# A new head for a two-layer transformer trunk: identity on chip, x and the first weights in quarters, fewer warm-up products

## The chip, the cores and the metric

The kernel runs on one core of one Trainium2 chip. A core has a matrix engine (TensorE, PE in the profile), a vector engine (VectorE, DVE), an activation engine (ScalarE, ACT), a general engine (GpSimd, POOL) and a sequencer that issues transfers (SyncE, SP); 16 DMA engines move data. The metric is the time of one launch on the device in microseconds (us), as the median of several runs. Lower is better.

## The reference

A trunk of two layers on 256 tokens of width 1024, all in float32. Each layer is a half SwiGLU sub-layer, a token-mixing sub-layer of two attentions, and another half SwiGLU. The change touches the first SwiGLU of the first layer alone:

```python
for l in range(DEPTH):                       # DEPTH = 2
    x = x + 0.5 * swiglu(rms_norm(x, ffn1_norm[l]), ffn1_w_gate[l], ffn1_w_up[l], ffn1_w_down[l])
    h = rms_norm(x, mix_norm[l])
    proj = h @ w_in[l]
    ...                                      # windowed attention A, latent attention B
    merged = sigmoid(g_a) * (o_a @ w_branch_a[l]) + sigmoid(g_b) * (o_b @ w_branch_b[l])
    x = x + merged @ w_out[l]
    x = x + 0.5 * swiglu(rms_norm(x, ffn2_norm[l]), ffn2_w_gate[l], ffn2_w_up[l], ffn2_w_down[l])

def swiglu(x, w_gate, w_up, w_down):         # D_FF = 2816
    return (silu(x @ w_gate) * (x @ w_up)) @ w_down
```

## The kernel before

Each engine has its own hand-written program, and the engines meet at semaphores. Every product of weights and activations is made in three float32r products: each operand is split into a rounded high part and the rest as a low part, and high times high, high times low and low times high are summed in PSUM. ScalarE makes the high parts (a copy that rounds), VectorE the low parts (a subtraction).

x lies in SBUF as two blocks of 128 tokens (t = 0, 1). For products it is needed transposed: TensorE transposes each 128x128 piece against an identity matrix (`ident`), two pieces (both t) for each of the eight column groups c. ScalarE reads the result from PSUM, multiplies with a gain from `cols` and writes the high part hTh (line 576, `columns_high`); VectorE writes the low part hTl (line 962, `columns_low`).

The gate and up weights of the feed-forward come in 22 blocks of 128 hidden columns. One block is 128 x 2048 floats (1 MB): 1024 columns for the gate and 1024 for up, each in eight pieces k = 0 to 7 that stand against the columns c of x.

The head, before any product can run:
- SyncE's queue carries, in this order, x of t = 0 (512 KB, line 301), the identity (line 302), the first weight block in two halves of 512 KB, gate and up (line 305), the second block in two halves (line 308), then the down weights of block 0 (line 332), the whole third block (line 344, into the tile SG) and the down weights of block 1. ScalarE's queue carries x of t = 1 (line 485) and the gains `cols` (line 486).
- TensorE runs 12 products of ones that nobody reads (`keep_warm`, line 1311), waits for the identity and both x blocks, and transposes all eight columns (`columns_start`, line 1325). Columns 6 and 7 reuse PSUM banks of columns 0 and 1 and wait for the low parts of those.
- ScalarE and VectorE alternate two columns of hT with one quarter of the first weight block (lines 521 and 872). Quarter, or piece, 0 is the gate's k = 0 to 3, piece 1 up's k = 0 to 3, pieces 2 and 3 are k = 4 to 7.
- TensorE follows in the same order (`gate_up_start`): for each piece two groups, each two high products of 512 columns and two low products of 256, all at line 1300 in the helper `mm`. Then come the second block (`gate_up_second`), in the middle of which two small products spread the inverse rms over the partitions (`spread_rs`), and the third block.
- GpSimd waits for x, and later takes the inverse root of the mean square (line 429, a power).

The order in which a program is written is the order in which its engine works; no planner moves it.

Of the kernel before, what the change touches and what calls it, by code (L numbers as in the profile page):

```python
# [14 lines left out]
P = 128  # L15
# [77 lines left out]
def build(nc, x_in, pos_in, cols_in, rows_in, w_ffn, w_proj, w_gate, w_uq, w_ukv, w_branch, w_out,  # L93
          masks_in, freq_in, out):
    with ExitStack() as ctx:
# [119 lines left out]
        start_in = [signal(f"start_in{i}", 0) for i in range(3)]  # L215
# [5 lines left out]
        ident_in = signal("ident_in", 0)  # L221
# [77 lines left out]
        def _(sp):  # L299
            x_tokens = x_in.rearrange("b (t p) d -> p (b t) d", p=P)  # L300
            sp.dma_start(x[:, 0, :], x_tokens[:, 0, :]).then_inc(x_in_done[0].sem, 16)
            sp.dma_start(ident[:, :], masks_in[0, :, 0:P]).then_inc(ident_in.sem, 16)
            for s in range(2):
                part = slice(s * KC * P, (s + 1) * KC * P)
                sp.dma_start(raw_gu[0][:, part], w_ffn[0, :, part]).then_inc(start_in[s].sem, 16)
            for s, sem in enumerate((start_in[2].sem, raw_gu_in[1].sem)):
                part = slice(s * KC * P, (s + 1) * KC * P)
                sp.dma_start(raw_gu[1][:, part], w_ffn[1, :, part]).then_inc(sem, 16)
# [88 lines left out]
        def _(pool):  # L397
# [4 lines left out]
            pool.memset(minus_half[:, :], -0.5).then_inc(half_set.sem, 1)  # L402
            pool.wait_ge(half_set.sem, 1)

            for t in range(TT):
                pool.wait_ge(x_in_done[t].sem, 16)
# [27 lines left out]
            pool.dma_start(maskA[:, :], masks_in[1]).then_inc(table_in.sem, 16)  # L434
            pool.dma_start(maskB[:, :], masks_in[2]).then_inc(table_in.sem, 16)
# [48 lines left out]
        def _(act):  # L484
            act.dma_start(x[:, 1, :], x_in.rearrange("b (t p) d -> p (b t) d", p=P)[:, 1, :]).then_inc(x_in_done[1].sem, 16)
            act.dma_start(cols[:, :], cols_in[0]).then_inc(small_in.sem, 16)
# [5 lines left out]
            for l in range(DEPTH):  # L492
# [25 lines left out]
                def start_high(i):  # L518

                    act.wait_ge(start_in[i % 2].sem, 16)  # L520
# [137 lines left out]
                if l == 0:  # L658
# [8 lines left out]
                    for s, (landed, sig) in enumerate(((start_in[2], start_hi), (raw_gu_in[1], hi_gu))):  # L667
# [155 lines left out]
        def _(dve):  # L823
# [3 lines left out]
            dve.wait_ge(ident_in.sem, 16)  # L827
# [470 lines left out]
        def _(pe):  # L1298
# [15 lines left out]
            keep_warm(12)  # L1314
            pe.wait_ge(ident_in.sem, 16)
            for l in range(DEPTH):
                def columns_start():

                    for t in range(TT):
                        pe.wait_ge(x_in_done[t].sem, 16)  # L1320
                    for c in range(KC):
# [69 lines left out]
                def gate_up_start():  # L1391

                    for half in range(2):
                        for s, sig in enumerate((gate_ps, gu_used)):
# [17 lines left out]
                            if half == 1:  # L1412
                                ins.then_inc(sig.sem, 1)

# [396 lines left out]
```

## Time and profile before

| | us |
|---|---|
| median of 3 runs | 1054.25 |
| lowest and highest run | 1053.63, 1054.94 |
| span of the profiled execution | 1051.9 |
| TensorE busy in that span | 1046.4 (99%) |
| VectorE busy | 721.1 (69%) |
| ScalarE busy | 593.3 (56%) |
| GpSimd busy | 66.0 (6%) |

The profile is of one execution. Its span runs from the first to the last instruction, and the time of a run contains 2.4 us more. Times in the views are us from the start of the span. The profile counts each warm-up product, a float32 product, as two records, and each transpose as one. "Idle before" in brackets names who ended the idle time of an engine. The granted clock of TensorE is recorded from 17.5 us of this trace on (the views show 1.00 for what lies before); before that the speed can be read from the durations and the spacing of equal instructions.

### The profile page before, as it was taken

How to read it: one execution, taken by the hardware profiler on the slowest of the kernel's cores; microseconds unless marked ns; L12 is line 12 of the kernel's file. 1: busy time of each engine (PE TensorE's matmuls, PEld its weight loads, DVE VectorE, ACT ScalarE, POOL GpSimd, SP SyncE). 2: the span in 40 equal slices, each digit the busy share in tenths (PEclk: the TensorE clock that was granted, in tenths of full speed). 3: DMA queues.
4: the chain of work that ended last, by engine and by line, in shares of the span. 5: the costliest groups of instructions: out<-in, count | busy, mean ns of one | idle time of the engine just before them, and what ended most of it. 6: DMA issues, size and time to landing. Idle time of an engine off the chain costs nothing.

```text
span 1051.9 us, 15566 instructions
## 1 busy us (share of the span) xinstructions
PE 1046.4 (99%) x5664; PEld 899.3 (85%) x5664; DVE 721.1 (69%) x1132; ACT 593.3 (56%) x931; POOL 66.0 (6%) x69
## 2 busy tenths in 40 slices
PE   9999999999999999999999999999999999999998
PEld 8888888898888888888888888889988888888887
DVE  6766666668786776666686666666697867666664
ACT  6555555467864655555565555555688556555552
POOL 1042000122100000000000000001211000000000
PEclk9999999999999999999999999999999999999999
DMA  7655554455335454555536445544454345554451
GB/s 261 242 203 200 202 193 144 139 180 209 126 121 200 151 209 179 182 196 203 199 136 224 180 179 182 196 166 133 157 203 158 116 165 191 208 199 180 179 182 58
DMA packets 35266, 187.55 MB, mean 178 GB/s; under 512 B 4496, under 2 KB 4640, under 8 KB 20128
## 3 DMA queue, kind: packets, MB, share of 16 engines
q1 hardware_dynamic: 34704, 186.03, 48.7%
q0 software_dynamic: 240, 0.53, 0.2%
q10 hardware_dynamic: 288, 0.54, 0.2%
q8 instruction: 20, 0.33, 0.1%
q14 instruction: 14, 0.11, 0.0%
HBM read 186.04 MB, written 1.05 MB: 178 GB/s over the span
## 4 chain that ended last, share of the span: by engine, by line
PE 99%; DVE 1%; issue 0%; ACT 0%; DVEq 0%; ACTq 0%
PE ps L1300 95%; PE ps L1337 1%; PE ps L1636 1%; PE ps L1311 1%; PE ps L1663 0%; PE ps L1699 0%; DVE x L955 0%; PE ps L1546 0%; DVE hT L962 0%; DVE S L1111 0%; PE ps L1538 0%; ACT hT L576 0%; PE ps L1325 0%; DVE w_lo L872 0%; DVE kTA L824 0%
## 5 line engine op out<-in xcount | busy, mean ns | idle before, releaser
L1300 PE MATMUL ps<-hT,w_hi 128*128 128x512 f32 x1408 | 355.4, 391 | 0.2 <-DVE hT L962 0.2
L1300 PEld LDWEIGHTS ps<-hT,w_hi 128*128 128x128 f32 x1408 | 256.3, 188 | 47.9 <-DVE hT L962 0.4
L839 DVE TENSOR_TENSOR w_lo<-w_raw,w_hi 128x2048 fp32r<-128x2048 f32 x82 | 187.9, 2292 | 73.3 <-ACT w_hi L516 73.3
L1300 PEld LDWEIGHTS ps<-hT,w_lo 128*128 128x128 f32 x1408 | 195.3, 190 | 16.0
L1300 PE MATMUL ps<-hT,w_lo 128*128 128x256 f32 x1408 | 200.0, 282 | 0.0
L1300 PE MATMUL ps<-w_hi,hT 128*128 128x512 f32 (+2 forms) x576 | 173.8, 377 | 0.0
L516 ACT ACTIVATE w_hi<-w_raw 128x2048 fp32r<-128x2048 f32 x85 | 162.3, 1910 | 18.5 <-PE ps L1300 13.2
L1300 PE MATMUL ps<-w_hi,aTh 128*128 128x512 f32 x352 | 138.2, 393 | 0.0
L1300 PE MATMUL ps<-w_lo,aTh 128*128 128x512 f32 x352 | 138.0, 392 | 0.0
L1300 PE MATMUL ps<-w_hi,aTl 128*128 128x512 f32 x352 | 137.0, 389 | 0.0
L919 DVE TENSOR_TENSOR S<-ps,S 128x256 f32<-128x256 f32 x88 | 37.3, 424 | 139.7 <-ACT S L557 139.7
L833 DVE TENSOR_TENSOR w_lo<-w_raw,w_hi 128x2048 fp32r<-128x2048 f32 (+3 forms) x54 | 101.2, 1883 | 34.6 <-ACT w_hi L504 34.6
L1300 PEld LDWEIGHTS ps<-w_hi,hT 128*128 128x128 f32 x576 | 107.4, 188 | 14.8
L504 ACT ACTIVATE w_hi<-w_raw 128x2048 fp32r<-128x2048 f32 (+3 forms) x54 | 86.0, 1593 | 55.1 <-PE ps L1300 53.0
L895 DVE TENSOR_TENSOR w_lo<-w_raw,w_hi 128x1024 fp32r<-128x1024 f32 x88 | 107.3, 1219 | 2.1 <-ACT w_hi L539 2.1
L1300 PE MATMUL ps<-w_lo,hT 128*128 128x512 f32 (+2 forms) x288 | 107.6, 374 | 0.0
L539 ACT ACTIVATE w_hi<-w_raw 128x1024 fp32r<-128x1024 f32 x88 | 93.4, 1062 | 19.1 <-PE ps L1300 19.1
L545 ACT ACTIVATE S<-ps 128x256 f32<-128x256 f32 x88 | 33.7, 383 | 121.0 <-PE ps L1300 121.0
L551 ACT ACTIVATE work<-work 128x256 f32<-128x256 f32 x88 | 36.7, 418 | 96.6 <-DVE work L908 96.6
L1300 PEld LDWEIGHTS ps<-w_hi,aTl 128*128 128x128 f32 x352 | 66.1, 188 | 14.5
L1300 PEld LDWEIGHTS ps<-w_hi,aTh 128*128 128x128 f32 x352 | 66.4, 189 | 12.1
L1300 PEld LDWEIGHTS ps<-w_lo,aTh 128*128 128x128 f32 x352 | 66.4, 189 | 10.5
(164 smaller groups left out, 961.7 us busy)
## 6 DMA issues: line engine op xcount, KB each, us to landing
w_raw<-in_w_ffn SPq DMA_DIRECT2D x85, 1024.0 KB, 5.4
w_raw<-in_w_ffn SPq DMA_DIRECT2D x92, 512.0 KB, 3.5
w_raw<-in_w_gate SPq DMA_DIRECT2D x16, 1024.0 KB, 4.9
w_raw<-in_w_proj SPq DMA_DIRECT2D x16, 592.0 KB, 4.4
w_raw<-in_w_branch SPq DMA_DIRECT2D x8, 1024.0 KB, 4.8
w_raw<-in_w_out SPq DMA_DIRECT2D x8, 1024.0 KB, 4.8
w_raw<-in_w_uq SPq DMA_DIRECT2D x4, 384.0 KB, 3.0
SG<-in_w_ffn SPq DMA_DIRECT2D x1, 1024.0 KB, 10.7
```

What stands on the lines that cost most here:

```text
L504: act.activation(mix_hi[m][:, 0:ncols], mix_raw[m][:, 0:ncols], ACT.Copy).then_inc(hi_gu.sem, 1)
L516: act.activation(wh_gu[b], raw_gu[b], ACT.Copy).then_inc(hi_gu.sem, 1)
L539: act.activation(wh_d[b], raw_d[b], ACT.Copy).then_inc(hi_d.sem, 1)
L545: act.activation(folded[:, b, 0, :], ps[:, 2 * b, SEQ:2 * SEQ], ACT.Copy).then_inc(g_low.sem, 1)
L551: act.activation(silu[:, b, :], silu[:, b, :], ACT.Silu).then_inc(silu_done.sem, 1)
L833: dve.tensor_tensor(mix_lo[m][:, 0:ncols], mix_raw[m][:, 0:ncols], mix_hi[m][:, 0:ncols].bitcast(F32), ALU.subtract).then_inc(lo_gu.sem, 1)
L839: dve.tensor_tensor(wl_gu[b], raw_gu[b], wh_gu[b].bitcast(F32), ALU.subtract).then_inc(lo_gu.sem, 1)
L895: dve.tensor_tensor(wl_d[b], raw_d[b], wh_d[b].bitcast(F32), ALU.subtract).then_inc(lo_d.sem, 1)
L919: dve.tensor_tensor(folded[:, b, 1, :], ps[:, 2 * b + 1, 0:SEQ], folded[:, b, 1, :], ALU.add)\
L1300: return pe.matmul(dst, w, m, start=start, stop=stop, skip_group_check=True)
L1311: pe.matmul(ps[:, 1, 0:P], kTA[:, 0:P], kTA[:, 0:P], start=True, stop=True, skip_group_check=True)
L1337: ins = pe.transpose(ps[:, X_BANK[c], c // 6 * SEQ + t * P:c // 6 * SEQ + (t + 1) * P], x[:, t, c * P:(c + 1) * P], ident[:, :])
```

## The change

- GpSimd makes the identity: it clears the tile and runs one `affine_select` that writes 1.0 on the diagonal. The identity is no longer loaded, and its page in the masks array is gone. VectorE no longer waits for it.
- x is loaded in four pieces of 256 KB. The left half (columns 0 to 3) of t = 0 is first on SyncE's queue, that of t = 1 first on ScalarE's; both right halves follow on ScalarE's queue. The gains move to SyncE's queue, second.
- The first weight block is loaded in four quarters of 256 KB, in the order of use.
- 7 warm-up products in place of 12.
- TensorE transposes columns 0 to 3, then runs piece 0 of the first block, and then transposes columns 4 to 7.

The arithmetic is the same. ScalarE and VectorE run the same operations in the same order as before.

```diff
@@ sync
-            sp.dma_start(x[:, 0, :], x_tokens[:, 0, :]).then_inc(x_in_done[0].sem, 16)
-            sp.dma_start(ident[:, :], masks_in[0, :, 0:P]).then_inc(ident_in.sem, 16)
-            for s in range(2):
-                part = slice(s * KC * P, (s + 1) * KC * P)
-                sp.dma_start(raw_gu[0][:, part], w_ffn[0, :, part]).then_inc(start_in[s].sem, 16)
-            for s, sem in enumerate((start_in[2].sem, raw_gu_in[1].sem)):
+            sp.dma_start(x[:, 0, 0:HALF], x_tokens[:, 0, 0:HALF]).then_inc(x_in_done[0].sem, 16)
+            sp.dma_start(cols[:, :], cols_in[0]).then_inc(small_in.sem, 16)
+            for i in range(4):
+                sp.dma_start(raw_gu[0][:, start_cols(i)], w_ffn[0, :, start_cols(i)]).then_inc(start_in[i].sem, 16)
+            for s, sem in enumerate((start_in[4].sem, raw_gu_in[1].sem)):
@@ gpsimd
             pool.memset(minus_half[:, :], -0.5).then_inc(half_set.sem, 1)
+            pool.memset(ident[:, :], 0.0).then_inc(ident_set.sem, 1)
+            pool.wait_ge(ident_set.sem, 1)
+            pool.affine_select(ident[:, :], ident[:, :], [[1, P]], ALU.not_equal, 1.0, base=0, channel_multiplier=-1)\
+                .then_inc(ident_set.sem, 1)
             pool.wait_ge(half_set.sem, 1)
-            for t in range(TT):
-                pool.wait_ge(x_in_done[t].sem, 16)
+            for h in range(2):
+                pool.wait_ge(x_in_done[h].sem, 32)
@@ scalar
-            act.dma_start(x[:, 1, :], x_in.rearrange("b (t p) d -> p (b t) d", p=P)[:, 1, :]).then_inc(x_in_done[1].sem, 16)
-            act.dma_start(cols[:, :], cols_in[0]).then_inc(small_in.sem, 16)
+            x_tokens = x_in.rearrange("b (t p) d -> p (b t) d", p=P)
+            act.dma_start(x[:, 1, 0:HALF], x_tokens[:, 1, 0:HALF]).then_inc(x_in_done[0].sem, 16)
+            for t in range(TT):
+                act.dma_start(x[:, t, HALF:], x_tokens[:, t, HALF:]).then_inc(x_in_done[1].sem, 16)
...
-                    act.wait_ge(start_in[i % 2].sem, 16)
+                    act.wait_ge(start_in[i].sem, 16)
@@ vector
-            dve.wait_ge(ident_in.sem, 16)
@@ tensor
-            keep_warm(12)
-            pe.wait_ge(ident_in.sem, 16)
+            keep_warm(7)
+            pe.wait_ge(ident_set.sem, 2)
...
-                def columns_start():
-
-                    for t in range(TT):
-                        pe.wait_ge(x_in_done[t].sem, 16)
-                    for c in range(KC):
+                def columns_start(h):
+
+                    pe.wait_ge(x_in_done[h].sem, 32)
+                    for c in range(4 * h, 4 * h + 4):
...
                             if half == 1:
                                 ins.then_inc(sig.sem, 1)
+                            if piece == 0:
+                                columns_start(1)
```

TensorE's order from its first instruction on, before; `kTA` is the tile of ones, `hT` holds the transposed x, x2 and the like is the number of equal instructions in a row:

```order
L1311 MATMUL ps<-kTA 128x128 x12
L1325 MATMUL ps<-ident,x 128x128 x16
L1300 MATMUL ps<-hT,w_hi 128x512 x2
L1300 MATMUL ps<-hT,w_lo 128x256 x2
L1300 MATMUL ps<-hT,w_hi 128x512 x2
L1300 MATMUL ps<-hT,w_lo 128x256 x2
L1300 MATMUL ps<-hT,w_hi 128x512 x2
```

TensorE's order at the same place now:

```order
L1315 MATMUL ps<-kTA 128x128 x7
L1328 MATMUL ps<-ident,x 128x128 x8
L1304 MATMUL ps<-hT,w_hi 128x512 x2
L1304 MATMUL ps<-hT,w_lo 128x256 x2
L1304 MATMUL ps<-hT,w_hi 128x512 x2
L1304 MATMUL ps<-hT,w_lo 128x256 x2
L1328 MATMUL ps<-ident,x 128x128 x8
L1304 MATMUL ps<-hT,w_hi 128x512 x2
```

Eight of the sixteen transposes moved behind the first two groups of products, those of piece 0.

SyncE's queue from the start, before; these are transfers, with their shape in floats:

```order
L301 DMA x<-in_x 128x1024
L302 DMA ident<-in_masks 128x128
L305 DMA w_raw<-in_w_ffn 128x1024 x2
L308 DMA w_raw<-in_w_ffn 128x1024 x2
L332 DMA w_raw<-in_w_ffn 128x1024
L344 DMA SG<-in_w_ffn 128x2048
```

SyncE's queue now:

```order
L301 DMA x<-in_x 128x512
L302 DMA cols<-in_gain_cols 128x31
L304 DMA w_raw<-in_w_ffn 128x512 x4
L307 DMA w_raw<-in_w_ffn 128x1024 x2
L331 DMA w_raw<-in_w_ffn 128x1024
L343 DMA SG<-in_w_ffn 128x2048
```

The identity and the right half of the first x block left this queue, the gains came to it, and the two halves of the first weight block are four quarters.

## Rows read from the trace of the kernel before

**Rows 1.** The page, section 4: shares of the chain that ended last, by engine.
```profile
PE 99%; DVE 1%; issue 0%; ACT 0%; DVEq 0%; ACTq 0%
```

**Rows 2.** That chain in order of time, to 30 us: start us, us, what.
```profile
1.05 5.49 PE ps L1311 x24
...
10.02 20.18 PE ps L1300 x111
```

**Rows 3.** Timeline, transfers issued: start us, us, queue, line, tile, count.
```profile
0.73 0.41 ACTq L485 DMA_DIRECT2D x<-in_x  x1
1.17 0.46 ACTq L486 DMA_DIRECT2D cols<-in_gain_cols  x1
1.65 0.42 SPq L305 DMA_DIRECT2D w_raw<-in_w_ffn  x1
4.16 0.45 SPq L344 DMA_DIRECT2D SG<-in_w_ffn  x1
```

**Rows 4.** Transfers in the order of rows 3: KB, us from issue to landing.
```profile
x<-in_x ACTq DMA_DIRECT2D x1, 512.0 KB, 5.0
cols<-in_gain_cols ACTq DMA_DIRECT2D x1, 15.5 KB, 5.0
w_raw<-in_w_ffn SPq DMA_DIRECT2D x1, 512.0 KB, 5.6
SG<-in_w_ffn SPq DMA_DIRECT2D x1, 1024.0 KB, 10.7
```

**Rows 5.** Windows: us, busy of PE, PEld, DVE, ACT, POOL, clock, DMA share, GB/s.
```profile
0.00:3.65 3.65, 2.60 (x12) 2.60 (x13) 0.18 (x2) 1.49 (x2) 0.31 (x5) 1.00 0.52 145
3.65:6.00 2.35, 2.35 (x13) 2.35 (x13) 0.00 (x0) 0.00 (x0) 0.00 (x0) 1.00 1.06 406
```

**Rows 6.** TensorE: line 1311 (ns min/median/max, first and last start), then the timeline.
```profile
L1311 PE MATMUL ps<-kTA x24: 421/421/581, 1.0 to 6.1; 128*128 128x128 f32 x24
...
6.33 2.74 PE L1325 MATMUL ps<-ident,x 128*128 128x128 f32 x16
...
6.97 0.50 PE L1325 MATMUL ps<-ident,x 128*128 128x128 f32 x3
...
10.82 0.62 PE L1300 MATMUL ps<-hT,w_hi 128*128 128x512 f32 x2
...
15.00 1.99 PE L1300 MATMUL ps<-hT,w_hi 128*128 128x512 f32 x8
...
18.93 0.61 PE L1300 MATMUL ps<-ident,rs 128*128 128x128 f32 x4
```

**Rows 7.** Timeline of ScalarE: start us, us, line, operation, tiles, shape.
```profile
7.09 0.84 ACT L576 ACTIVATE hT<-ps,cols 128x256 fp32r<-128x256 f32 x2 [3.93 <-PE ps L1325]
7.82 0.63 ACT L521 ACTIVATE w_hi<-w_raw 128x512 fp32r<-128x512 f32 x1
...
9.05 0.65 ACT L521 ACTIVATE w_hi<-w_raw 128x512 fp32r<-128x512 f32 x1
...
15.50 2.07 ACT L529 ACTIVATE w_hi<-SG 128x1024 fp32r<-128x1024 f32 x2
```

**Rows 8.** Timeline of VectorE.
```profile
7.70 0.88 DVE L962 SCALAR_TENSOR_TENSOR hT<-ps,cols,hT 128x256 fp32r<-128x256 f32 x2 [6.69 <-ACT hT L576]
...
9.09 0.87 DVE L962 SCALAR_TENSOR_TENSOR hT<-ps,cols,hT 128x256 fp32r<-128x256 f32 x2
...
10.47 0.88 DVE L962 SCALAR_TENSOR_TENSOR hT<-ps,cols,hT 128x256 fp32r<-128x256 f32 x2
...
12.64 0.69 DVE L872 TENSOR_TENSOR w_lo<-w_raw,w_hi 128x512 fp32r<-128x512 f32 x1
```

**Rows 9.** GpSimd: its timeline, then groups by line and shape (busy us, mean ns).
```profile
16.09 1.62 POOL L429 TENSOR_TENSOR rs<-rs_step,minus_half 128x2 f32<-128x2 f32 x1 [14.86 <-DVE rs_step L889]
...
L449 POOL TENSOR_SCALAR S<-S,posq 128x128 f32<-128x128 f32 x1 | 0.6, 613 | 0.1
...
L479 POOL TENSOR_TENSOR small<-small,minus_half 128x16 f32<-128x16 f32 x4 | 15.6, 3889 | 50.7 <-DVE small L1161 36.6 <-DVE small L1203 14.1
```

More of the change, by code:

```diff
@@ L214, in build @@
         x_in_done = [signal(f"x_in_done{h}", 0) for h in range(2)]
-        start_in = [signal(f"start_in{i}", 0) for i in range(3)]
+        start_in = [signal(f"start_in{i}", 0) for i in range(5)]
         third_in = signal("third_in", 0)
@@ L220, in build @@
         third_lo = signal("third_lo", 0)
-        ident_in = signal("ident_in", 0)
+        ident_set = signal("ident_set", 0)
         table_in = signal("table_in", 0)
@@ L433, in _ @@
             pool.wait_ge(a_lo.sem, a_lo.at(0, 5))
-            pool.dma_start(maskA[:, :], masks_in[1]).then_inc(table_in.sem, 16)
-            pool.dma_start(maskB[:, :], masks_in[2]).then_inc(table_in.sem, 16)
+            pool.dma_start(maskA[:, :], masks_in[0]).then_inc(table_in.sem, 16)
+            pool.dma_start(maskB[:, :], masks_in[1]).then_inc(table_in.sem, 16)
             pool.dma_start(freq[:, :], freq_in).then_inc(table_in.sem, 16)
@@ L666, in _ @@
                     start_high(3)
-                    for s, (landed, sig) in enumerate(((start_in[2], start_hi), (raw_gu_in[1], hi_gu))):
+                    for s, (landed, sig) in enumerate(((start_in[4], start_hi), (raw_gu_in[1], hi_gu))):
                         part = slice(s * KC * P, (s + 1) * KC * P)
@@ L1465, in ffn @@
                     if l + w == 0:
-                        columns_start()
+                        columns_start(0)
                     else:
@@ L1780 @@
     zero = np.zeros((P, P), f32)
-    eye = np.concatenate([np.eye(P, dtype=f32), zero, zero], axis=1)
     two = lambda g: np.concatenate([g, g], axis=1)
@@ L1800 @@
         "w_out": a["w_out"].reshape(L, 4, 2, P, D_MODEL).transpose(0, 1, 3, 2, 4).reshape(4 * L, P, GU_COLS),
-        "masks": np.stack([eye, np.concatenate([causal, previous, causal], axis=1),
+        "masks": np.stack([np.concatenate([causal, previous, causal], axis=1),
                            np.concatenate([causal, zero, causal], axis=1)]),
```

## Prediction

> **What bounds the kernel now.** The shares of the chain of waits come first: 99% of the chain that ended last is TensorE [rows 1]. The chain in order of time comes second [rows 2]. It starts with the 24 records of the 12 warm-up products at 1.05 us. From 10.02 us on it is TensorE's products without a gap as far as I followed it. So after 10.02 us the kernel is fixed work on one engine. An edit of the head can only move the moment at which that work has no more holes, and each us so moved is a us of the total. I use the start of the second weight block's products, at 15.00 us, as the mark [rows 6]: all work of the head lies before it, the same work in both kernels apart from warm-ups. Then the landings (issue time plus time to landing) [rows 3, 4], then the rhythm of each engine [rows 6 to 8].
>
> Before the change TensorE transposes x from 6.33 us on, with no idle time in front [rows 6]. The second x part landed at 0.73 + 5.0 = 5.73 us [rows 3, 4], and the identity did not hold TensorE either, since nothing shows between warm-ups and transposes. So the warm-ups fill the wait for x, with 0.6 us at most beyond it.
>
> **Part 1: seven warm-ups.** 24 records take 6.33 - 1.05 = 5.28 us, 0.22 us each. 14 take 3.08 us, so TensorE is free at **4.13 us**.
>
> **Part 2: x in quarters on two queues.** The first halves of both row blocks are 512 KB, in place of 1024 KB. Between 3.65 and 6 us 406 GB/s were moved [rows 5], so 512 KB cost 1.29 us. The columns 0 to 3 land at about 5.73 - 1.29 = 4.44; I take **4.5 us**, since descriptors are half as long. From below: at 3.65 us 145 x 3.65 = 529 KB had been moved [rows 5], so 3.7 us is the earliest even without delay of the signal, and then the warm-ups end last, at 4.13. The gain columns (cols) came 1.17 + 5.0 - 5.73 = 0.44 us behind the x part ahead of them on their queue [rows 3, 4]. Now that is 4.9 us at the latest, and ScalarE needs them after the first two transposes, at 5.2. Hidden. Transposes start at 4.5 in place of 6.33: **1.8 us earlier**.
>
> **Part 3: identity on GpSimd.** No row shows an affine select. GpSimd's nearest operation of that size, a 128x128 scalar operation, took 0.61 us; far above stands its power on 128x16, 3.89 us [rows 9]. It starts after two memsets at some 1.5 us. By the first row the identity is there near 2.5 us and hidden under 4.5; by the second at 5.4 or more, and each us beyond 4.5 is paid once. I take the first, since a select is plain elementwise work. Below nothing it can't go: the identity did not hold TensorE before. What queues behind it on GpSimd is the first power, at 16.09 us. Dropping DVE's wait for the identity is worth nothing, as DVE's first product comes at 7.70 us [rows 8].
>
> **Part 4: first weight block in quarters.** Quarter 0 ends behind 1024 KB of x and weights plus cols, so at about what x took before, 5.8 us. ScalarE wants it 1.8 us earlier than at 7.82, at 6.0 [rows 7]. Quarter 1 ends behind 1552 KB; the first weight half landed at 1.65 + 5.6 = 7.25 behind about 1616 KB, so 7.1 us, and ScalarE wants it at 9.05 - 1.8 = 7.25. Both are just in time. Quarters 2 and 3 follow 0.65 us apart (7.8, 8.4), long before their use. The second x halves share the two queues with quarters 0 and 1, so they land at about 7.1 us too.
>
> **Part 5: columns 4 to 7 behind piece 0.** This takes most of the gain back. Follow TensorE, everything 1.8 us early at first. The first two low columns of hT are done at 8.58 - 1.8 = 6.8, and piece 0 starts. Its second half needs the low columns 2 and 3, done at 9.96 - 1.8 = 8.15 [rows 8]. It takes one group of products: the six groups from 10.82 to 15.00 took 0.70 us each [rows 6]. Piece 0 ends at 8.9. Only now come the eight transposes. At full clock they stand 0.11 us apart (three records in 0.50 us, the last of them 0.27 long) [rows 6], 0.86 us in all, until 9.75. Before, they ran while VectorE was making its first columns. The second cost is on ScalarE: it is through with quarter 1 at 7.25 + 0.6 = 7.9 and has no column 4 before 9.2, so some 1.3 us of idle time. VectorE follows 0.6 us behind ScalarE (7.09 against 7.70) and starts column 4 at about **10.0, against 10.47** before [rows 8]. From there it runs its old, unbroken rhythm, **0.45 us early** in place of 1.8.
>
> TensorE again: piece 1 from 9.75 to 11.15; piece 2's first group to 11.85; its second needs low column 7, which was ready at about 12.7 and is now at 12.25, a wait of 0.4; it ends at 12.95, and piece 3 (low weights ready at 13.33 - 0.45 = 12.9) at 14.35. The mark moves from 15.00 to about 14.4: **0.6 us gained**. The sum once more: 1.8 earlier, less 0.86 of transposes no longer beside other work, less 0.4 of new waiting; rounding leaves 0.55 to 0.6.
>
> Does it last? The power on GpSimd ended at 16.09 + 1.62 = 17.71 [rows 9] and moves 0.45 us; the product that spreads it stood at 18.93 [rows 6] and moves 0.6. Still a us of room. The third block landed at 4.16 + 10.7 = 14.86 [rows 3, 4] with the queues full until then, and the total of bytes hardly changes. ScalarE took it up at 15.50 [rows 7], now 14.9 to 15.05. Just met. Its products stand behind two whole blocks on TensorE, so a small delay there costs nothing.
>
> **The clock.** The warm-up records take 421 ns and stand 0.22 us apart; the first transposes stand just so, (6.97 - 6.33) / 3 = 0.21 us; from 6.97 us on they stand 0.11 us apart [rows 6]. So TensorE left its lower level (1.2 GHz) for 2.4 GHz at about 7.0 us, after 5.9 us of work without a hole. No granted clock is recorded that early. Now it idles between 4.13 and 4.5 and again before piece 0 (5.9 or 6.2 to 6.8) and inside it. The Trainium skill, "TensorE: Matmul & The Clock Gate", section "What's actually happening", says that the default state is the throttled one and that activity releases it; the trace of the kernel before agrees, with full speed only from about 7.0 us. By that rule fewer warm-ups and new holes can put the rise off; that is the rival C, priced by rows. In my sum the clock rises near 7 us as before. Cold transposes cost nothing: four columns cold take 1.7 us, and the first low columns come at 6.8.
>
> **The rivals.**
> A, the forecast: 0.6 us gained, 1053.6. If quarter 0 or 1 lands 0.5 us late, or the x half at 4.9, it is 0.1; if all lands early, 1.1. Own range 1053.0 to 1054.3. Chance 0.57.
> B, the transfers bound: the four small pieces share the engines so that the x half lands no earlier than 5.2 us, or quarter 1 after 8. Then nothing is gained: 1054.0 to 1054.8, chance 0.10. For it: 0.25 us of room for the quarters. Against it: the two queues moved 406 GB/s together.
> C, the clock rises late, slower than before. Until about 8.4 us cold products hide in waits for VectorE. After that each us at the lower level costs half a us, so from a rise at 9.6 us on the gain of 0.6 is gone. At 10.4 us it is 0.4 us slower (1054.7), at 13.8 us 2.7 - 0.6 = 2.1 slower (1056.4). For it: the holes. Against it: before 10.02 us the chain ran over ScalarE and VectorE, so TensorE had holes there too [rows 2], and it kept its speed: two products of 512 columns in 0.62 us at 10.82 [rows 6]. Chance 0.23, a fifth of it beyond 2.1 us.
> D, the identity is late: decides from 4.5 us on (a select of over 2.9 us), one for one, less the 0.6 gained. With 3.9 us for it, 1054.7; chance 0.05.
> E, more than said: x at 4.1 and ScalarE's idle time smaller, 1.1 to 2.2 us gained. 2.2 is the end, since the transposes can't start before 4.13. 1052.6, chance 0.05.
>
> **How the numbers follow.** The sum is made on a profiled execution with a span of 1051.9 us; the median of the three runs is 1054.25, 2.4 us more, which the edits don't touch (and the runs differ by 1.3 us among themselves). The forecast is 1054.25 - 0.6 = **1053.6**. The range takes in A, B, most of C and D, and most of E: **1052.5 to 1055.5**. About 0.2%, 2.1 us, is what a measurement of this kernel can tell from no change. Faster by more needs nearly all of the 2.2 of E: 0.04. Slower by more needs the far end of C or a very slow select: 0.06. Within: 0.90.
>
> **What would show it.** In the new profile: the first transposes at 4.5 us; the second eight near 8.9; ScalarE idle for over a us ahead of column 4 and waiting for TensorE's transposes; VectorE's column 4 near 10.0; the second block near 14.4; spacing of 0.11 us in the second transposes (0.21 would be C). Wrong is the sum if the transposes wait for GpSimd, if ScalarE waits for a weight quarter by over 0.3 us, or if a hole stands in TensorE's row after 15 us.

## The result and the profile after

| | median us | runs | lowest, highest | span of the profiled execution |
|---|---|---|---|---|
| before | 1053.7 | 21 | 1052.97, 1054.94 | 1051.9 |
| changed | 1055.33 | 21 | 1054.27, 1057.19 | 1053.5 |

The changed kernel is **slower by 1.6 us: ratio 1.0016, 95% interval 1.0010 to 1.0022**. The forecast was 0.6 us faster. It is within 0.2%, but on the other side of nothing, and clear of the noise of 21 runs. 1055.33 lies inside the stated range of 1052.5 to 1055.5, close to its upper end; that is luck, since the sum behind the forecast went the other way.

The chain of waits of the changed kernel, in order of time (start us, us, what), answers to [rows 2]:

```profile
1.65 5.64 DMA w_raw<-in_w_ffn
...
7.32 0.64 ACT w_hi L526
...
8.00 3.16 PE ps L1304 x8
11.16 1.71 PE ps L1328 x8
12.87 7.31 PE ps L1304 x41
```

Warm-ups are gone from the chain. What stands at its head now is a transfer, weight quarter 0 (issued at 1.65 us), then ScalarE's high part of it, and then TensorE without a gap, from 8.00 us in place of 10.02. So TensorE has its last gap 2 us earlier and still ends later. The next lines are the timelines of TensorE, ScalarE, VectorE and GpSimd, with idle time and its releaser in brackets, and answer to [rows 6 to 9]:

```profile
5.29 1.94 PE L1328 MATMUL ps<-ident,x 128*128 128x128 f32 x8 [0.88 <-DMA x<-in_x]
8.00 1.22 PE L1304 MATMUL ps<-hT,w_hi 128*128 128x512 f32 x2 [0.77 <-ACT w_hi L526]
...
9.51 1.22 PE L1304 MATMUL ps<-hT,w_hi 128*128 128x512 f32 x2
...
10.96 1.91 PE L1328 MATMUL ps<-ident,x 128*128 128x128 f32 x8
...
17.00 1.99 PE L1304 MATMUL ps<-hT,w_hi 128*128 128x512 f32 x8
```

```profile
7.32 0.63 ACT L526 ACTIVATE w_hi<-w_raw 128x512 fp32r<-128x512 f32 x1 [0.41 <-DMA w_raw<-in_w_ffn]
...
11.68 0.84 ACT L581 ACTIVATE hT<-ps,cols 128x256 fp32r<-128x256 f32 x2 [2.19 <-PE ps L1328]
```

```profile
12.26 0.88 DVE L966 SCALAR_TENSOR_TENSOR hT<-ps,cols,hT 128x256 fp32r<-128x256 f32 x2 [2.04 <-ACT hT L581]
```

```profile
1.64 0.28 POOL L404 TENSOR_SCALAR_AFFINE_SELECT ident<-ident 128x128 f32<-128x128 f32 x1 [0.26 <-POOL ident L402]
```

To be seen:
- The first transposes start at 5.29 us, held by x, and the second eight at 10.96, behind piece 0.
- Two products of 512 columns take 1.22 us at 8.00 and at 9.51, where [rows 6] has 0.62 us: TensorE is at its lower level (1.2 GHz). The second transposes too: eight in 1.91 us, 0.21 us apart. Full speed comes at 13.0 us, in place of 7.0.
- ScalarE stands idle for 2.19 us ahead of column 4, VectorE for 2.04. In this execution that costs nothing by itself, as TensorE has no gap behind it.
- Piece 0 starts 0.8 us earlier than before (8.00 against 8.82), and from there to the second block TensorE takes 9.0 us in place of 6.2. The 2.8 us more are: piece 0's two groups 2.96 us in place of 2.00, the eight transposes that now stand there 1.56 us, and the six groups behind them 4.48 in place of 4.18. In e5 below, at full speed, the same eight transposes take 0.8 us. So about half of the 2.8 us is the low clock and not the order.
- The second block starts at **17.00 us against 15.00**, and the span is 1.7 us longer. From there the two traces are the same: span less mark is 1036.5 us here and 1036.9 before. In all seventeen traces of this study it lies between 1036.5 and 1037.4. So the start of the second block, the mark of the prediction, tells the span of an execution to within 0.9 us. The time of a run adds 1.8 to 2.1 us to the span in the median of each kernel here, except e5 (2.6).
- The select on GpSimd took 0.28 us and was done at 1.9.

The landings, from the view of transfers (KB, us from issue to landing). The left halves of x, the left half of t=1 on ScalarE's queue first; then quarter 0, issued at 1.65 us:

```profile
x<-in_x ACTq DMA_DIRECT2D x1, 256.0 KB, 3.9
x<-in_x SPq DMA_DIRECT2D x1, 256.0 KB, 4.4
...
w_raw<-in_w_ffn SPq DMA_DIRECT2D x1, 256.0 KB, 5.6
...
x<-in_x ACTq DMA_DIRECT2D x1, 256.0 KB, 6.5
```

The left halves were complete at 0.73 + 3.9 = 4.6 us on ScalarE's queue and 0.74 + 4.4 = 5.15 us on SyncE's, quarter 0 at 7.3, the last right half at 1.66 + 6.5 = 8.2 us.

One correction: the section on the profile before says that the granted clock is recorded from 17.5 us on, and the prediction that none is recorded so early. Counted from the start of the span, the first record is at 7.0 us, and it is the rise itself.

### The profile page after: what moved, and what is told of

The parts are those of the page before. It is cut to its first block, busy times and chain, and to the rows that moved or that the text cites. A ratio compares the mean times of both kernels' runs of the same rounds, so it can differ in the third digit from the quotient of the medians.

```text
span 1053.5 us, 15551 instructions
## 1 busy us (share of the span) xinstructions
PE 1046.8 (99%) x5654; PEld 899.6 (85%) x5654; DVE 721.1 (68%) x1132; ACT 593.7 (56%) x931; POOL 65.8 (6%) x71
## 3 DMA queue, kind: packets, MB, share of 16 engines
HBM read 185.97 MB, written 1.05 MB: 178 GB/s over the span
## 4 chain that ended last, share of the span: by engine, by line
PE 99%; DMA 1%; DVE 0%; SPq 0%; issue 0%; DVEq 0%; ACT 0%
PE ps L1304 95%; PE ps L1340 1%; PE ps L1641 1%; DMA w_raw<-in_w_ffn 1%; PE ps L1668 0%; PE ps L1704 0%; PE ps L1551 0%; DVE x L959 0%; PE ps L1328 0%; DVE S L1115 0%; PE ps L1543 0%; DVEq L95 0%; ACT w_hi L526 0%; SPq L302 0%; SPq L301 0%
## 5 line engine op out<-in xcount | busy, mean ns | idle before, releaser
L1304 PEld LDWEIGHTS ps<-hT,w_lo 128*128 128x128 f32 x1408 | 195.9, 191 | 16.2 <-DVE w_lo L876 0.2
L1304 PEld LDWEIGHTS ps<-w_hi,hT 128*128 128x128 f32 x576 | 107.4, 188 | 14.8
```

Of the source, the lines that this page charges most:

```text
L1304: return pe.matmul(dst, w, m, start=start, stop=stop, skip_group_check=True)
```

## The experiments

Three suspects: the **clock** (C), the **order** of transposes and piece 0 (O), the **transfers** in pieces (Q). The change has all three, so most kernels undo or do one. All were compared with the kernel before on the same chip. "Mark" is the start of the second block, "quarter 0" its landing (of the kernels with halves, the gate half), "rise" the clock's first rise, all from the one profiled execution; the median is over 10 or 11 runs.

| kernel | median us (before's) | ratio, 95% interval | mark | quarter 0 | rise |
|---|---|---|---|---|---|
| before | 1053.7 | | 15.0 | 7.2 | 7.0 |
| changed | 1055.33 (1053.7) | 1.0016, 1.0010 to 1.0022 | 17.0 | 7.3 | 13.0 |
| e1: changed, 12 warm-ups | 1054.72 (1053.51) | 1.0012, 1.0002 to 1.0021 | 16.6 | 8.0 | 5.5 |
| e2: before, 7 warm-ups | 1053.84 (1053.51) | 1.0006, 0.9996 to 1.0015 | 15.0 | 7.7 | 4.5 |
| e3: changed, old order | 1053.73 (1053.51) | 1.0001, 0.9992 to 1.0010 | 16.9 | 8.0 | 12.8 |
| e4: changed, old order, 12 warm-ups | 1053.61 (1053.51) | 1.0001, 0.9992 to 1.0011 | 14.2 | 7.0 | 4.6 |
| e5: before, new order | 1055.18 (1053.51) | 1.0017, 1.0007 to 1.0027 | 16.2 | 7.5 | 6.1 |
| e6: before, identity on GpSimd | 1054.35 (1053.45) | 1.0008, 0.9999 to 1.0017 | 15.3 | 7.1 | 6.3 |
| e7: e6 with 10 warm-ups | 1054.44 (1053.51) | 1.0008, 0.9999 to 1.0017 | 15.4 | 7.0 | 4.9 |
| e8: changed, 10 + 2 warm-ups | 1054.45 (1053.45) | 1.0009, 1.0000 to 1.0018 | 18.0 | 8.6 | 5.8, fell at 9.2, rose at 12.6 |
| e9: e4 with another queue order | 1053.96 (1053.51) | 1.0004, 0.9995 to 1.0013 | 14.8 | 7.3 | 5.2 |
| e10: transposes within piece 0 | 1054.70 (1053.51) | 1.0011, 1.0002 to 1.0020 | 14.8 | 6.9 | 8.8 |
| e11: x whole, gains on SyncE | 1053.30 (1053.45) | 1.0000, 0.9991 to 1.0009 | 14.5 | 6.6 | 4.8 |
| e12: changed, again | 1057.4, one run (1053.45) | | 18.5 | 8.3 | 4.8, fell at 8.2, rose at 15.0 |
| e13: right halves behind quarters | 1054.36 (1053.56) | 1.0006, 0.9997 to 1.0015 | 15.2 | 5.7 | 5.2 |
| e14: e13 with old order | 1054.08 (1053.56) | 1.0008, 0.9999 to 1.0017 | 14.6 | 5.7 | 5.1 |
| e15: halves first, then quarters | 1053.80 (1053.56) | 1.0004, 0.9995 to 1.0013 | 14.7 | 7.5 | 6.8 |

A profile is one execution of the eleven, and not always a middle one: that of e8 is its slowest run and that of e3 too, that of e4 is its fastest and that of e10 its second fastest. So the medians carry the verdicts and the traces the mechanisms. The profile of before is not a middle one either: its span is 1051.9 us, and the median span of before's runs was 1051.4 to 1051.6 on the four chips of e1 to e15. Its mark of 15.0 is thus 0.3 to 0.5 us late; an estimate for a typical execution, from these spans less 1036.9, is 14.5 to 14.7.

**The order alone: e5.** `columns_start` in two calls on the kernel before, nothing else.

```diff
                             if half == 1:
                                 ins.then_inc(sig.sem, 1)
+                            if piece == 0:
+                                columns_start(1)
```

> The kernel before with one thing changed: columns 4 to 7 are transposed behind piece 0 of the first block. Transfers, identity and 12 warm-ups as before, so the clock rises near 7 us. Theory O (the order costs by itself): piece 0 ends at 10.8 us, column 4 reaches ScalarE at 11.3 in place of 9.6 and VectorE at 11.9 in place of 10.5, and the second block starts at 16.3 us in place of 15.0: 1.3 us over before (1055.0). Rival: the transposes fit into TensorE's waits there and it is within 0.3 us of before.

Measured: 1.67 us over before, the largest effect of any single part, with the clock high from 6.1 us on. By the spans it is less, 1052.65 against 1051.6 us in the median: time less span is 2.6 us in e5 and 1.8 in before, and no view shows where these 0.7 us lie. TensorE's and ScalarE's timelines:

```profile
9.76 0.73 PE L1300 MATMUL ps<-hT,w_hi 128*128 128x512 f32 x2 [0.29 <-DVE hT L962]
...
10.57 1.04 PE L1325 MATMUL ps<-ident,x 128*128 128x128 f32 x8
...
13.97 0.73 PE L1300 MATMUL ps<-hT,w_hi 128*128 128x512 f32 x2 [0.26 <-DVE hT L962]
...
16.18 1.32 PE L1300 MATMUL ps<-hT,w_hi 128*128 128x512 f32 x5
```

```profile
11.05 0.84 ACT L576 ACTIVATE hT<-ps,cols 128x256 fp32r<-128x256 f32 x2 [1.58 <-PE ps L1325]
```

x was complete at 5.9 us in this execution, and ScalarE waited 1.58 us for a transpose that could have been made at 7.1. VectorE waited 1.32 us in turn, and piece 2 of the products then waited for VectorE. Theory O holds, at 1.2 us of the mark and 1.05 of the span where 1.3 were expected.

**Undoing the order: e3 and e4.** The changed kernel with both `columns_start` calls ahead of piece 0; e4 has 12 warm-ups besides.

```diff
-                            if piece == 0:
-                                columns_start(1)
...
                         columns_start(0)
+                        columns_start(1)
```

> The changed kernel (new transfers, identity on GpSimd, 7 warm-ups), with all eight columns transposed ahead of piece 0 as before. Theory O (the order is the loss): as with 12 warm-ups and this order, the second block starts at 14.2 to 15.0 us and the time is that of before within 0.3 us (1053.2 to 1053.9). Theory C (the low clock under 7 warm-ups is the loss): the time stays over before by a us or more in the median (1054.5 or more), with a second block at 15.5 to 17 us wherever the clock rises late.

> The changed kernel with the 12 warm-ups and the transpose order of before (all eight columns ahead of piece 0): what is left of the change is the transfers in pieces and the identity on GpSimd. If the new transfers cost what the trace of the changed kernel suggests (quarter 0 at 7.3, second x halves at 8.2, quarter 1 at 8.85 us), columns 4 to 7 are transposed at 8.2 to 9.0 us, VectorE starts column 4 at 10.2 to 10.5, and the second block starts within 0.3 us of 15.0: the same as before, 1053.4 to 1054.0. If the transfers are the whole loss (theory Q), it is 1055 or more.

Neither can be told from before. The order costs 1055.33 - 1053.73 = 1.6 us with 7 warm-ups (the runs of before on that chip were 0.2 us faster) and 1054.72 - 1053.61 = 1.1 us with 12. Three pairs with e5, 1.1 to 1.7 us of time and 1.05 to 1.6 of span: **in the median the order is the loss**. And e4 says that the new transfers and the identity on GpSimd together gain nothing, though x lands earlier.

The profiled execution of e3 shows where this ends. It is the slowest of its eleven, with the clock low until 12.8 us and the last right half landing at 8.2:

```profile
8.27 1.97 PE L1328 MATMUL ps<-ident,x 128*128 128x128 f32 x8 [1.07 <-DMA x<-in_x]
9.89 1.20 PE L1304 MATMUL ps<-hT,w_hi 128*128 128x512 f32 x2
...
16.91 0.62 PE L1304 MATMUL ps<-hT,w_hi 128*128 128x512 f32 x2
```

Its mark is 16.9 with the old order, against 17.0 in the trace of the changed kernel, and both runs took 1055.32 us. In this pair, with TensorE itself slow, the order hardly matters. The traces alone could not have told order from clock; the medians and e5 do.

**The clock: e1, e2, e8 and e12.** e1 is one number:

```diff
-            keep_warm(7)
+            keep_warm(12)
```

> The changed kernel with 12 warm-up products again, all else as changed. Theory C (the lower clock until 13.0 us is what costs): with TensorE busy until 6.33 us the clock rises near 7 us as in the kernel before, piece 0 still starts at 8.0 us behind its weight quarter, its two groups then take 0.7 us in place of 1.5, and the second block starts near 15.9 us in place of 17.0: 1054.2 us in all. Theory Q (only the late transfers cost): the clock is hidden behind the waits for weights, the second block stays at 17.0 us or later, 1055.3 us or more.

e2 is the other way round, on the kernel before:

```diff
-            keep_warm(12)
+            keep_warm(7)
```

> The kernel before with 7 warm-up products in place of 12, nothing else. TensorE then stands idle from 4.1 us until the identity lands at 6.0. Theory C: the clock rises at 13 us as in the changed kernel; 16 cold transposes end at 9.4 us, 2.8 groups of products run at 1.3 us each until 13.0 and the rest at 0.7, so the second block starts at about 16.6 us in place of 15.0, and the time is 1.6 us over before (1055.3). Theory Q: the clock rises where it did, the transposes start 0.35 us earlier, and the time is 0.3 us under before (1053.4).

e1 is 0.6 us under the changed kernel (0.4, each against its own before) and still 1.2 over before. The two intervals overlap, so the price of the warm-ups is less sure than that of the order; with the old order it is 0.1 us (e3 against e4). In the trace of e1 the rise came at 5.5 us and piece 0 started at 8.7, as quarter 0 landed at 8.0. e2 is 0.3 us over before, with an interval that holds zero. In its profiled execution the clock rose at 4.5 us, behind 7 products. So 7 warm-ups don't fix the rise at 13 us; it differs from one execution to the next. The second trace of the changed kernel shows the other bad case:

> The changed kernel once more, for its trace alone. Theory C says that the moment of the clock's rise differs between executions with 7 warm-ups (13.0 and 8.8 and 4.5 us in the traces so far); the start of the second block follows it, between 16.0 and 17.0 us. If the late clock is fixed to this order of work, it rises near 13 us again and the second block starts at 17.0.

Windows of it (us, busy of PE, PEld, DVE, ACT, POOL, then the granted clock):

```profile
5.00:7.00 2.00, 1.06 (x8) 0.86 (x8) 0.54 (x2) 0.84 (x2) 0.00 (x0) 1.00 1.03 360
7.00:9.00 2.00, 0.04 (x1) 0.04 (x1) 0.40 (x2) 0.72 (x2) 0.00 (x0) 0.80 1.06 405
9.00:11.00 2.00, 2.00 (x5) 1.57 (x6) 2.00 (x4) 1.15 (x3) 0.00 (x0) 0.50 1.03 416
11.00:13.00 2.00, 2.00 (x10) 1.84 (x9) 0.01 (x1) 0.36 (x1) 0.00 (x0) 0.50 1.06 438
13.00:15.00 2.00, 2.00 (x9) 1.81 (x8) 1.78 (x4) 2.00 (x6) 0.00 (x0) 0.50 0.97 403
15.00:17.00 2.00, 2.00 (x13) 1.73 (x13) 1.88 (x4) 2.00 (x3) 0.00 (x0) 1.00 0.46 186
```

TensorE was at 2.4 GHz by 4.8 us, stood idle from 6.4 to 8.96 because quarter 0 landed late, fell to 1.2 GHz at 8.2 while idle, and stayed there until 15.0 us, over all of piece 0, the second transposes and the first products of piece 1. The mark is 18.5 and the run 1057.4. The expectation (a mark between 16.0 and 17.0) was too narrow: it had no second fall in it. Of 21 timed runs of the changed kernel 8 had a mean clock of 0.999 or less; of the 10 of e1 none. That mean doesn't see a late first rise (it is 1.0 in the profiled run, with its rise at 13.0), and the eight have a median only 0.15 us over the other thirteen, so it counts falls and gives no price. The trace bears out the Trainium skill, "TensorE: Matmul & The Clock Gate", section "What's actually happening", on the point that activity releases the throttle, and shows its other side: the wait that the change leaves before piece 0 can bring it back.

e8 tried to close the holes: 10 products, and 2 more behind the first eight transposes.

```diff
-            keep_warm(7)
+            keep_warm(10)
...
                         columns_start(0)
+                        keep_warm(2)
```

> The changed kernel with 10 warm-up products in place of 7 and 2 more behind the first eight transposes, so that TensorE has no hole before piece 0 (some 0.2 us later with its first transposes, nothing else). Theory C: the clock rises by 7 us in every execution; with the order's cost left, the time is that of the changed kernel with 12 warm-ups, 1054.5 to 1054.9, and the spread of runs is under 1.5 us. Rival: the holes don't matter and the time is that of the changed kernel, 1055.3.

Its median is 1054.45, as e1 within the noise. Each against its own before, e1 and e8 are 0.4 and 0.6 us better than the changed kernel (0.6 and 0.9 in the plain medians); the intervals overlap with that of the changed kernel, so this is the likely price of the clock and not a shown one. The spread of under 1.5 us was not reached: one run, the profiled one, took 1057.15. In it the fillers ended at 7.1 us, quarter 0 came at 8.6, and the clock fell at 9.2 and rose again at 12.6. Filler products sized for an early landing don't cover a late one.

**The place of the transposes: e10.** One group earlier, inside piece 0, where TensorE waits for VectorE:

```diff
-                            if piece == 0:
-                                columns_start(1)
...
                                     ins = low(s, wl_gu[0][:, c:c + P], k, k == KC - 1)
+                                if piece + k0 == 0:
+                                    columns_start(1)
```

> The changed kernel with the transposes of columns 4 to 7 one group of products earlier, between the two groups of piece 0, where TensorE waits for the low columns 2 and 3 anyway. Theory O: column 4 reaches ScalarE about 1 us earlier (near 10.5 in place of 11.5 to 11.7), the second block starts 0.8 to 1.1 us earlier, and the time is 1054.2 to 1054.6 in place of 1055.3. Theory C: the clock decides and the place of the transposes moves nothing: 1055.2 to 1055.5.

0.6 us under the changed kernel in the median, less than expected, and runs between 1053.15 and 1056.08. In its trace column 4 reached ScalarE at 9.5 and the mark was 14.8, but there the clock also rose at 8.8; order and clock can't be told apart in this one. It points the same way as O, no more.

**Why quarter 0 was late: e9, e13, e14.** e9 dealt the pieces to the queues in another order (x right half of t=1 and quarter 0 on SyncE's, right half of t=0 and quarter 1 on ScalarE's), with 12 warm-ups and the old order of transposes:

```diff
-            for i in range(4):
+            for i in (0, 2, 3):
                 sp.dma_start(raw_gu[0][:, start_cols(i)], w_ffn[0, :, start_cols(i)]).then_inc(start_in[i].sem, 16)
+                if i == 0:
+                    sp.dma_start(x[:, 1, HALF:], x_tokens[:, 1, HALF:]).then_inc(x_in_done[1].sem, 16)
...
-            for t in range(TT):
-                act.dma_start(x[:, t, HALF:], x_tokens[:, t, HALF:]).then_inc(x_in_done[1].sem, 16)
+            act.dma_start(x[:, 0, HALF:], x_tokens[:, 0, HALF:]).then_inc(x_in_done[1].sem, 16)
+            act.dma_start(raw_gu[0][:, start_cols(1)], w_ffn[0, :, start_cols(1)]).then_inc(start_in[1].sem, 16)
```

> Transposes all ahead and 12 warm-ups, with the pieces in another order on the queues: SyncE's carries x left half of t=0, the gains, weight quarter 0, x right half of t=1, quarters 2 and 3; ScalarE's x left half of t=1, x right half of t=0, quarter 1. Theory Q (quarter 0 and the right halves are late because ScalarE's queue holds 768 KB of x and is served ahead): quarter 0 lands 0.5 us or more earlier (near 6.5 in place of 7.0 to 8.0) and the second block starts at 13.8 to 14.2 us: 0.3 us under before. Rival: the landings stay within 0.3 us of those with the old order, since the sum of bytes decides, and the time is that of before.

Quarter 0 came at 7.3, not 6.5, and the left halves at 5.6: the rival. The time is 0.45 us over before, with an interval that holds zero. e9 left open whether the right halves or the pieces as such are at fault. e13 moves the right halves out of quarter 0's way, onto SyncE's queue behind quarters 0 and 1, and has 10 warm-ups:

```diff
             for i in range(4):
                 sp.dma_start(raw_gu[0][:, start_cols(i)], w_ffn[0, :, start_cols(i)]).then_inc(start_in[i].sem, 16)
+                if i == 1:
+                    for t in range(TT):
+                        sp.dma_start(x[:, t, HALF:], x_tokens[:, t, HALF:]).then_inc(x_in_done[1].sem, 16)
...
-            for t in range(TT):
-                act.dma_start(x[:, t, HALF:], x_tokens[:, t, HALF:]).then_inc(x_in_done[1].sem, 16)
```

> The changed kernel (column order included) with 10 warm-ups, and with the right halves of x on SyncE's queue behind quarters 0 and 1 in place of ScalarE's queue, which then holds one left half alone. Theory Q (quarter 0 is late in the changed kernel because the right halves share the engines with it): quarter 0 lands near 5.9 to 6.2 us, 1 us or more earlier, quarter 1 near 6.7, the right halves near 8.0; piece 0 starts near 7.0 and the second block at 14.6 to 15.0 us, as the forecast's own sum has it with those landings: 1053.2 to 1053.7. Rival: SyncE's queue alone doesn't fill the engines, quarter 0 lands near 7 again, and the time is that with 12 warm-ups, 1054.5 to 1054.9.

Quarter 0 now landed 4.0 us after its issue at 1.65, in place of 5.6:

```profile
w_raw<-in_w_ffn SPq DMA_DIRECT2D x1, 256.0 KB, 4.0
```

That is 5.7 us, and quarter 1 at 6.3. The trace of e14, with the same transfers, has 5.7 too. Theory Q is right on the landing: it was the right halves on the other queue. TensorE and VectorE in the trace of e13:

```profile
5.35 1.04 PE L1329 MATMUL ps<-ident,x 128*128 128x128 f32 x8
7.50 0.70 PE L1305 MATMUL ps<-hT,w_hi 128*128 128x512 f32 x2 [1.11 <-DVE hT L967]
...
9.60 1.03 PE L1329 MATMUL ps<-ident,x 128*128 128x128 f32 x8
...
15.21 1.99 PE L1305 MATMUL ps<-hT,w_hi 128*128 128x512 f32 x8
```

```profile
10.66 0.88 DVE L967 SCALAR_TENSOR_TENSOR hT<-ps,cols,hT 128x256 fp32r<-128x256 f32 x2 [1.32 <-ACT hT L582]
```

Even so the mark is 15.2, not 14.6 to 15.0, and the median 0.8 us over before: VectorE has its old hole of 1.32 us in front of column 4. The pair e14 has both `columns_start` calls ahead of piece 0, as e4:

> The same transfers and warm-ups with all columns transposed ahead of piece 0. Now TensorE waits for the right halves (near 8.0 us) before any product: piece 0 starts at 9.0. Theory O in its general form (a step placed behind a late transfer costs what the transfer is late): second block at 14.9 to 15.3, 0 to 0.3 us over before (1053.5 to 1053.8). This is where the changed order should be at least as good as the old one: the pair differs by under 0.3 us, against 1.1 to 1.6 with the right halves early.

1054.08 against 1054.36: the order costs 0.3 us here, as expected (0.7 on the marks, 14.6 and 15.2). Both lie 0.5 to 0.8 us over before, more than expected. What differs from the other pairs is that quarter 0 (5.7 us) comes over 2 us ahead of the last right half (8.0 and 8.2); with the changed kernel's queues they land within 0.2 to 1.1 us of each other in seven traces. Transposing late costs little where the step put ahead has its data much earlier.

**The identity and the gains: e6 and e7.** Only the load of the identity is replaced by GpSimd's select (e7: and 10 warm-ups):

```diff
-            sp.dma_start(ident[:, :], masks_in[0, :, 0:P]).then_inc(ident_in.sem, 16)
...
+            pool.memset(ident[:, :], 0.0).then_inc(ident_set.sem, 1)
+            pool.wait_ge(ident_set.sem, 1)
+            pool.affine_select(ident[:, :], ident[:, :], [[1, P]], ALU.not_equal, 1.0, base=0, channel_multiplier=-1)\
+                .then_inc(ident_set.sem, 1)
```

> The kernel before with one thing changed: the identity is made on GpSimd and not loaded. Theory L: without that load the gains land late (7.4 us in the one trace of it with 10 warm-ups, against 6.2), ScalarE starts near 7.5 in place of 7.1, and the time is 0.4 to 0.9 us over before. Rival: that landing was a single event, and the time is that of before within 0.2 us.

> The kernel before with the identity made on GpSimd (no load of it) and 10 warm-up products in place of 12; x whole on two queues, weight halves and transposes as before. Transposes start at 5.85 us, when x has landed, in place of 6.33. If TensorE's start is what the head hangs on: 0.4 us under before (1053.1). If the first weight half (landed at 7.2 to 7.7 us, and taken up by ScalarE at 7.8) is: the same as before. If the clock rises later for the missing products, up to 0.5 us over before.

Both are 0.9 us over before, a surprise for an edit that takes a transfer away; the intervals touch zero, so the size is less sure than the sign. The trace of e6 points at the gains on ScalarE's queue:

```profile
cols<-in_gain_cols ACTq DMA_DIRECT2D x1, 15.5 KB, 6.1
```

6.1 us in place of 5.0 [rows 4], with x complete at the same time, and ScalarE starts at 7.34 in place of 7.09. The mark is 0.3 us later than in the trace of before, so the two traces account for a third of the 0.9 us. Packets of that queue (q10) in the stretch from 5.5 to 7.0 us, first before, then e6:

```profile
q10 hardware_dynamic: 2, 0.00, 0.1%
```

```profile
q10 hardware_dynamic: 123, 0.01, 6.4%
```

Before, the gains' 128 packets of 124 bytes went by while the other queue held the identity's small ones, of 512 bytes. Without the identity the other queue holds 4 KB pieces of weights, and the gains' packets take 1.1 us longer. That the two queues take turns packet by packet fits both counts; it was not tried by itself. In e7 the gains took 6.2 us. In the changed kernel the gains stand on SyncE's queue and came at 5.3 us.

**Meant to beat both: e11 and e15.** e11: x whole on two queues, gains on SyncE's, quarters, identity on GpSimd, 10 warm-ups, old order.

```diff
-            sp.dma_start(x[:, 0, 0:HALF], x_tokens[:, 0, 0:HALF]).then_inc(x_in_done[0].sem, 16)
+            sp.dma_start(x[:, 0, :], x_tokens[:, 0, :]).then_inc(x_in_done[0].sem, 16)
...
-            act.dma_start(x[:, 1, 0:HALF], x_tokens[:, 1, 0:HALF]).then_inc(x_in_done[0].sem, 16)
-            for t in range(TT):
-                act.dma_start(x[:, t, HALF:], x_tokens[:, t, HALF:]).then_inc(x_in_done[1].sem, 16)
+            act.dma_start(x[:, 1, :], x_tokens[:, 1, :]).then_inc(x_in_done[0].sem, 16)
...
-            keep_warm(7)
+            keep_warm(10)
```

> Meant to beat both: identity on GpSimd, gains on SyncE's queue, weight quarters, 10 warm-ups, but x whole on two queues and all columns transposed first. x lands at 5.7 to 5.8, the gains near 6.1, quarter 0 near 6.6; transposes from 5.85, ScalarE from 6.6 in place of 7.1, second block at 14.4 to 14.6 us: 0.4 to 0.5 us under before (1053.1). Rival: a landing in this stretch moves later by as much, and it is the same as before.

e15 keeps x in halves, with one right half on each queue ahead of all weights; else as e11:

```diff
             sp.dma_start(cols[:, :], cols_in[0]).then_inc(small_in.sem, 16)
+            sp.dma_start(x[:, 0, HALF:], x_tokens[:, 0, HALF:]).then_inc(x_in_done[1].sem, 16)
...
-            for t in range(TT):
-                act.dma_start(x[:, t, HALF:], x_tokens[:, t, HALF:]).then_inc(x_in_done[1].sem, 16)
+            act.dma_start(x[:, 1, HALF:], x_tokens[:, 1, HALF:]).then_inc(x_in_done[1].sem, 16)
```

> Meant to beat both: x in halves on both queues (left halves, the gains, then right halves, one each per queue), then the weight quarters, identity on GpSimd, 10 warm-ups, all columns transposed first. Left halves at 5.1, gains 5.4, right halves 6.3, quarter 0 near 6.9; transposes from 5.3, ScalarE from 6.0 and waiting 0.2 us for quarter 0; second block at 14.2 to 14.4 us: 0.6 us under before (1052.9). Rival: quarter 0 over 7.4 us, and the same as before.

e11 had its landings as expected (quarter 0 at 6.6) and a mark of 14.5, and its median is 0.15 us under before, with a ratio of 1.0000: better than the changed kernel, not shown to be better than before. e15 had quarter 0 at 7.5 and is the same as before: its rival.

## Why the prediction was wrong, point by point

The steps that failed are three terms of the sum: the landing of the left halves (part 2), the landing of quarter 0 (part 4), and the clock, put at nothing. The first two left 0.8 us of the head start at piece 0 where the sum had 2.0 (8.00 and 6.8, against 8.82 before), so that the loss through the order, which the sum had nearly right, stood alone. The clock made it larger in the trace.

- **What bounds the kernel** and the mark: right. The span follows the mark to within 0.9 us.
- **Part 1**, warm-ups end at 4.13: nearly right (14 records, over at 4.4), and hidden behind x. Its price on the clock was put at nothing; see below.
- **Part 2**, left halves at 4.5 us: wrong. They landed at 5.15 (5.1 to 5.2 in every trace with this transfer order). The bytes halved and the landing moved 0.6 us, not 1.29, and the first transposes 1.0 us, not 1.8. The step that failed is the pricing by the full rate of 406 GB/s [rows 5]. Up to 3.65 us the changed kernel moved even less than the 145 GB/s of before:

```profile
0.00:3.65 3.65, 2.60 (x12) 2.60 (x13) 0.18 (x2) 1.49 (x2) 0.73 (x7) 1.00 0.38 93
```

The half on ScalarE's queue did come near the forecast, at 4.6 us; SyncE's moved by 0.3 us alone, from 5.4 to 5.15, and in e13, without the right halves on the other queue, it was there at 5.1. What holds that one back stays open.
- **Part 3**, identity hidden: right in the changed kernel, 0.28 us. The prediction did not see that taking its load away moves other transfers (e6).
- **Part 4**, quarter 0 at 5.8: wrong, and dearer. It landed at 7.3, and at 6.9 to 8.6 in the other traces with this queue order. The prediction had it "just in time" with 0.2 us of room, and its count of bytes put just 768 KB of x and weights beside it. e13 gave 5.7 for the same piece with the right halves out of the way: the number was right for a layout that the change doesn't have. Piece 0 was forecast at 6.8 and started at 8.0, held by quarter 0.
- **Part 5**, the order takes most of the gain back: the mechanism is right and its size too. e13 is the check, a trace with early quarters and a high clock: first transposes 5.35 in place of 4.5, and from there everything 0.6 to 0.85 us behind the forecast, at 9.60 (8.9), 10.66 (10.0) and 15.21 (14.35). The loss through the order was put at 1.26 us (0.86 + 0.4); e5 measured 1.2 on the mark. What was wrong is the other side of the balance: 1.8 us of head start on paper, and in e4, which has the new transfers and the old order, a median 0.1 us over before.
- **The clock**: rival C named the mechanism. For a rise at 13.0 us, as in the first trace, its rule of half a us for each us after 8.4 gives 2.3 us. In the trace, piece 0 and the eight transposes take 4.5 us (8.00 to 12.52) and in e5 at full speed 3.0 (8.35 to 11.36), which is 1.5. In the median it is likely 0.4 to 0.9 us (e1, e8), and e12 lies 2.1 us over the median of the changed kernel. The prediction kept the rise near 7 us because the engine had kept its speed over holes before; the hole that the trace of before shows, ahead of 10.02 us, is 0.24 us long. The holes ahead of the first transposes and of piece 0 are 0.9 and 0.8 us now, and the second is 2.6 us in e12, because of the late quarter.
- **The rivals**: B (transfers bound, nothing gained) and C came together. B alone was given 0.10 and C 0.23, as if exclusive. They aren't: in e12 and e8 the late quarter makes the hole that the clock falls into. B with the order's full cost is not "nothing gained" either but slower, since part 5's loss stays when part 2's gain goes. That is the combination to price: 0 gained, less 1.2 for the order, less 0.6 for the clock. It gives 1.8 us, and 1.6 were measured; with prices taken from the experiments this is a sum made afterwards and no test.

What stays open: why quarter 0 lands anywhere between 6.9 and 8.6 us in executions of one transfer order, how often the changed kernel's clock rises late, and what makes up the rest of the 0.9 us of e6 and e7. That e14 is not faster than before with a mark of 14.6 in its trace is no riddle: its profiled execution has one of its three shortest spans (1051.3 us, median 1052.0), and 14.6 is what a typical execution of before has too.

## What to carry to other kernels

Price the two sides of a reordering apart: what it loses can be read from the old trace (1.26 us forecast, 1.2 measured in e5), what it gains hangs on landings, and if the gain is a transfer's, ask what the forecast is with that gain at zero. Work moved behind a waiting step costs every engine that feeds on it, here 1.1 to 1.7 us in three pairs, and 0.3 us where its data came over 2 us later than those of that step. Warm-up products cover a wait only if they last until the data are there in a slow execution too.

## What the runs showed of the hardware

- The clock can rise, fall and rise again in the first 15 us: 4.8, 8.2, 15.0 us in e12, with TensorE idle from 6.4 to 8.96. With 7 warm-ups the first rise lay at 4.5, 4.8, 8.8, 12.8 and 13.0 us in five traces; with 10 or more at 4.6 to 7.0 in all twelve, though in e8 it fell again at 9.2.
- Halving the first transfer from 512 KB to 256 KB on each of two queues brought the later of the two 0.6 us earlier (5.15 against 5.73 us), less than half of the 1.29 us that the bytes take at 406 GB/s. ScalarE's moved by 1.1 us, SyncE's by 0.3.
- A transfer of 15.5 KB in 128 pieces took 6.1 and 6.2 us beside 4 KB pieces on the other queue (e6, e7) and 5.0 us beside small ones (before).
- A 256 KB piece on SyncE's queue took 4.0 us with one left half alone on ScalarE's queue (e13, e14), and 5.2 to 6.9 us with the two right halves there as well.
- An affine select of 128x128 on GpSimd took 0.28 us, as the first and only one at the start of the kernel.
